# Turning input and output tiles of a one-layer decoder step with VectorE block transposes instead of TensorE transposes

## The reference

```
h  = rmsnorm(x) ; z = h @ w_in                       # 2048 x 10240, columns for r k v g u g_pool gate_a gate_b
decay = exp(-0.6065 * sigmoid(w0 + tanh(xw @ w1) @ w2))   # low rank 96, xw mixes h and the previous row
a     = sigmoid(a0 + (xa @ a1) @ a2)                      # low rank 96
S, o  = wkv7_scan(...)                               # 16 heads of 64
m  = sigmoid(gate_a) * (y_a @ w_branch[0]) + sigmoid(gate_b) * (y_b @ w_branch[1])
x  = x + rmsnorm(m @ w_out)                          # 2048 x 2048
x  = x + sigmoid(x @ w_ple_gate) * (p @ w_ple)       # 2048 x 2048 and 256 x 2048
return x (tokens as rows), states
```

## Time and profile before

| | |
|---|---|
| median of 3 runs | 1179.3 us (1177.43 to 1180.31) |
| profiled execution | 1180.21 us, span 1178.6 us |
| mean granted TensorE clock | 0.993 of full speed |
| TensorE busy | 1155.0 us (98%) |
| VectorE busy | 788.6 us (67%) |
| ScalarE busy | 531.7 us (45%) |

### The profile page before, as it was taken

One profiled execution on the slowest core, in us unless ns is written; L12 is line 12 of the kernel. 1 busy time (PEld: TensorE's weight loads), 2 busy tenths in 40 slices (PEclk: granted clock), 3 DMA queues, 4 the chain that ended last, 5 costly groups with the idle time before them and its releaser, 6 DMA issues.

```text
span 1178.6 us, 22183 instructions
## 1 busy us (share of the span) xinstructions
PE 1155.0 (98%) x7876; PEld 1122.9 (95%) x7876; DVE 788.6 (67%) x1689; ACT 531.7 (45%) x906; POOL 149.8 (13%) x251
## 2 busy tenths in 40 slices
PE   6979999999999999999999999999999999999998
PEld 6869999999999999999999999999999999989998
DVE  5977898989888888888679644444444444475442
ACT  5434564646463646455363333333333433354332
POOL 2322130303012121311050000000000400000000
PEclk9989999999999999999999999999999999999999
DMA  9713343434334344333364555545555954425551
GB/s 240 186 36 102 109 110 107 111 107 111 107 99 120 98 119 117 101 108 99 113 184 124 161 144 157 145 143 158 144 151 151 280 161 139 133 69 142 165 164 47
DMA packets 279707, 155.08 MB, mean 132 GB/s; under 512 B 7717, under 2 KB 275661, under 8 KB 279012
## 3 DMA queue, kind: packets, MB, share of 16 engines
q1 hardware_dynamic: 272528, 139.65, 42.2%
q0 software_dynamic: 6992, 14.87, 4.9%
q10 hardware_dynamic: 148, 0.04, 0.0%
HBM read 149.15 MB, written 5.61 MB: 131 GB/s over the span
## 4 chain that ended last, share of the span: by engine, by line
PE 94%; DVE 3%; DMA 1%; issue 1%; POOL 0%; ACT 0%; SPq 0%; DVEq 0%; ACTq 0%; POOLq 0%
PE acc L1722 20%; PE acc L1723 19%; PE acc L1724 19%; PE wide L1724 5%; PE wide L1723 5%; PE wide L1722 5%; PE wide L1741 2%; PE wide L1823 1%; PE wide L2113 1%; PE wide L1877 1%; PE wide L1858 1%; DVE wl L1089 1%; PE wide L1864 1%; DMA xt<-in_x_prompt 1%; PE wide L1945 1%; PE wide L1869 1%
## 5 line engine op out<-in xcount | busy, mean ns | idle before, releaser
L1089 DVE TENSOR_TENSOR wl<-wraw,wh 128x1024 fp32r<-128x1024 f32 x256 | 316.9, 1244 | 196.2 <-ACT wh L708 194.2
L708 ACT CAST wh<-wraw 128x1024 fp32r<-128x1024 f32 x256 | 267.0, 1049 | 214.2 <-PE acc L1724 128.5
L1722 PE MATMUL acc<-hh,wh 128*128 128x320 f32 (+1 forms) x1084 | 349.5, 322 | 1.9 <-DVE hl L1175 1.9
L1723 PE MATMUL acc<-hl,wh 128*128 128x320 f32 (+1 forms) x1084 | 337.5, 311 | 0.0
L1724 PE MATMUL acc<-hh,wl 128*128 128x320 f32 (+1 forms) x1084 | 336.9, 311 | 0.0
L1722 PEld LDWEIGHTS acc<-hh,wh 128*128 128x128 f32 x1084 | 205.3, 189 | 2.7 <-DVE hl L1175 2.4
L1723 PEld LDWEIGHTS acc<-hl,wh 128*128 128x128 f32 x1084 | 205.0, 189 | 0.2
L1724 PEld LDWEIGHTS acc<-hh,wl 128*128 128x128 f32 x1084 | 204.9, 189 | 0.0
L1722 PE MATMUL acc<-x1h,wh 128*128 128x320 f32 x256 | 81.0, 316 | 0.0
L1722 PE MATMUL acc<-mh,wh 128*128 128x320 f32 x256 | 80.5, 315 | 0.0
L1724 PE MATMUL acc<-x1h,wl 128*128 128x320 f32 x256 | 79.1, 309 | 0.0
(11 more groups left out here) (422 smaller groups left out, 2100.6 us busy)
## 6 DMA issues: line engine op xcount, KB each, us to landing
wraw<-in_w_in SPq DMA_DIRECT2D x160, 512.0 KB, 3.8
wraw<-in_w_branch SPq DMA_DIRECT2D x32, 512.0 KB, 3.9
wraw<-in_w_out SPq DMA_DIRECT2D x32, 512.0 KB, 4.0
wraw<-in_w_ple_gate SPq DMA_DIRECT2D x32, 512.0 KB, 4.1
xt<-in_x_prompt SPq DMA_DIRECT2D x2, 1024.0 KB, 7.4
S0n<-in_state_wkv POOLq DMA_DIRECT2D x64, 32.0 KB, 4.5
out<-so POOLq DMA_DIRECT2D x16, 128.0 KB, 3.6
xt<-in_x_prompt POOLq DMA_DIRECT2D x2, 1024.0 KB, 6.9
```

Source lines behind the costliest of these rows:

```text
L708: A.copy(wh[:, slot, :], wraw[:, slot, :]).then_inc(s["hi_ready"], 1)
L1089: V.tensor_tensor(wl[:, slot, :], wraw[:, slot, :], wh[:, slot, :].bitcast(F32), ALU.subtract).then_inc(s["lo_ready"], 1)
L1722: M.matmul(out[:, 0:width], wh[:, slot, wcol], hi, start=first, stop=False)
L1723: M.matmul(out[:, 0:width], wh[:, slot, wcol], lo, start=False, stop=False)
```

## The change

It has three parts. In the start stage the first head pair's decay maps become two plain fp32 matmuls, `lora_high(0)` and `lora_low(0)` go, and VectorE's order changes. In the out stage x is turned by 40 VectorE block transposes (a 32-row quadrant by 16 k tiles by 32 columns each), three ahead of each out tile i = 2..14 and one ahead of the last, and neither TensorE nor ScalarE takes part any more (the embedding's two tiles stay with them, ahead of the last two out tiles). In the gate stage each `yo` is turned into `ytk` by sixteen VectorE block transposes right behind it; `tokens` and `token_tile` go. The stores stay where they are on SyncE and wait for sixteen block transposes. Before it writes `ytk[:, m]`, VectorE waits that all earlier stores out of it have landed.

```diff
+BLOCK_MOVES = [(a, q, r) for a in range(3) for q in range(4 if a < 2 else 2) for r in range(4)]
+TURNED = {i: BLOCK_MOVES[3 * (i - 2):3 * (i - 1)] for i in range(2, KT)}
...
             def store(i, m):
-                sp.wait_ge(s["ytk_ready"], i * 2 + 2)
+                sp.wait_ge(s["ytk_ready"], i * 16 + 16)
...
         @block.scalar
-            lora_high(0)
...
             decays(0)
             gates(4)
+            act.wait_ge(s["filled"], 2 + 10)
...
                 act.wait_ge(s["chunk_used"], i * 2 + (BASE_GATE + 2))
+                act.wait_ge(s["yo_ready"], i - 1)
                 A.activation(g3[:, m, :], acc[m][:, 0:T], ACT.Sigmoid).then_inc(s["g3_ready"], 1)
...
         @block.vector
+            values_turned(0, 3)
+            decays(0)
             dve.wait_ge(s["filled"], 2 + 10)
             states_turned(0)
             dve.wait_ge(s["lora_tok"], 4)
+            dve.wait_ge(s["lora2_ps"], 1)
             V.tensor_tensor(t1_l[:, :], t1[:, :], t1_h[:, :].bitcast(F32), ALU.subtract).then_inc(s["lora_lo"], 1)
             V.tensor_tensor(la_l[:, :], la[:, :], la_h[:, :].bitcast(F32), ALU.subtract).then_inc(s["lora_lo"], 1)
-            lora_low(0)
-            values_turned(0, 3)
-            decays(0)
...
+            def turned_blocks(a, q, r):
+                rows_q, rows_r = slice(BLK * q, BLK * (q + 1)), slice(BLK * r, BLK * (r + 1))
+                V.transpose(xTv[rows_r, :, P * a + BLK * q:P * a + BLK * (q + 1)],
+                            xt2[rows_q, a, :].rearrange("p (k d) -> p k d", d=P)[:, :, rows_r]).then_inc(s["x_turned"], 1)
+            dve.wait_ge(s["x2_in"], 48)
+            for i in range(2, KT):
+                for move in TURNED[i]:
+                    turned_blocks(*move)
+                out_tile(i // 2, i % 2)
...
                 V.tensor_tensor(yo[:, m, :], g3[:, m, :], xT[:, ds(n * (2 * T) + m * T, T)], ALU.add).then_inc(s["yo_ready"], 1)
+                if not first:
+                    dve.wait_ge(s[f"y_out{m}"], n * 32)
+                dve.wait_ge(s["yo_ready"], i + 1)
+                for q in range(4):
+                    n_tiles = 3 if q < 2 else 2
+                    for r in range(4):
+                        V.transpose(ytk[BLK * q:BLK * (q + 1), m, 0:P * n_tiles].rearrange("p (a d) -> p a d", d=P)[:, :, BLK * r:BLK * (r + 1)],
+                                    token_blocks(m, q, n_tiles)[BLK * r:BLK * (r + 1)]).then_inc(s["ytk_ready"], 1)
...
         @block.tensor
-            decay_maps(0)
+            pe.wait_ge(s["lw2_in"], 32)
+            pe.wait_ge(s["lora_tok"], 2)
+            M.matmul(B[0][:, 0:T], lw2[:, :], t1[:, :], start=True, stop=True)
+            M.matmul(B[1][:, 0:T], la2[:, :], la[:, :], start=True, stop=True).then_inc(s["lora2_ps"], 1)
...
             with pe.Fori(2, KT // 2) as n:
-                gate_tile(n, 0)
-                tokens(n * 2 - 1, 1, n * 4 - 4)
-                gate_tile(n, 1)
-                tokens(n * 2, 0, n * 4 - 2)
-            tokens(KT - 1, 1, 2 * KT - 4)
+                for m in range(2):
+                    pe.wait_ge(s["g3_ready"], n * 2 + m - 1)
+                    gate_tile(n, m)
```

More of the change, by code:

```diff
@@ L370, in build @@
         wple = r5.take("wple", [P, 2, 2 * P])
-        yo = r5.take("yo", [P, 2, T])
+        yo_wide = r5.take("yo_wide", [P, 2, 3 * P])
+        yo = yo_wide[:, :, 0:T]
         emb = at(used["ml"][0], "emb", [P, EMB, T])
@@ L1010, in _ @@
                 act.wait_ge(s["sacc_ready"], i - 1)
-                for u in TURNED[i]:
-                    turned_tile(u)
+                if i >= KT - 2:
+                    turned_embedding(i - (KT - 2))
                 square_tile(i // 2, i % 2)
@@ L1050, in gate_tile @@
                 act.wait_ge(s["chunk_used"], i * 2 + (BASE_GATE + 2))
+                act.wait_ge(s["yo_ready"], i - 1)
                 A.activation(g3[:, m, :], acc[m][:, 0:T], ACT.Sigmoid).then_inc(s["g3_ready"], 1)
[L1053 to L1059, removed]
             first_gate(0)
             first_gate(1)
-            token_tile(0, 0)
             gate_tile(1, 0)
-            token_tile(1, 1)
             gate_tile(1, 1)
-            token_tile(2, 0, 32)
             with act.Fori(2, KT // 2 - 1) as n:
-                gate_tile(n, 0)
-                token_tile(n * 2 - 1, 1, n * 32 - 32)
-                gate_tile(n, 1)
[L1072 to L1078, removed]
+                for m in range(2):
+                    gate_tile(n, m)
+            for m in range(2):
+                gate_tile(KT // 2 - 1, m, last=True)
         @block.vector
@@ L1651, in _ @@
             out_tile(0, 1)
-            with dve.Fori(1, KT // 2) as n:
-                for m in range(2):
-                    out_tile(n, m)
+            xTv = xT[:, :].rearrange("p (k t) -> p k t", t=T)
+            def turned_blocks(a, q, r):
[7 more added lines that the diff above has]
+                out_tile(i // 2, i % 2)
+            dve.wait_ge(s["x_turned"], len(BLOCK_MOVES))
             def gate_ahead(j):
@@ L2073, in _, with turned_embedding @@
             sizes = (P, P, NB * TB)
[L2075 to L2089, removed]
+            def turned_embedding(k):
+                pe.wait_ge(s["pool_in"], 64)
+                for t in range(3):
+                    last = transpose(B[4 + k][:, P * t:P * t + sizes[t]], pt[0:sizes[t], t, P * k:P * (k + 1)])
+                last.then_inc(s["pT_ps"], 1)
             for i in range(2, KT):
-                for u in TURNED[i]:
-                    turned_tile(u)
+                if i >= KT - 2:
+                    turned_embedding(i - (KT - 2))
                 out_tile(i // 2, i % 2, True)
@@ L2098, in gate_tile @@
                     chunk(n * 4 + BASE_GATE, 2 * m + h, acc[m], x1h, x1l, T, T, KC * h, h == 0, h == 1)
-            def tokens(i, m, free):
-                pe.wait_ge(s["yo_ready"], i + 1)
-                if free is not None:
-                    pe.wait_ge(s["ytk_ready"], free)
-                for t in range(3):
-                    last = transpose(B[2 + m][0:sizes[t], P * t:P * (t + 1)], yo[:, m, P * t:P * t + sizes[t]])
-                last.then_inc(s["yt_ps"], 1)
             def embedding(i):
@@ L2141, in _ @@
                 chunk(BASE_GATE, 4 + h, acc[0], x1h, x1l, T, T, KC * h, h == 0, h == 1)
[L2142 to L2144 removed]
+            pe.wait_ge(s["g3_ready"], 2)
             gate_tile(1, 1)
[L2146 removed]
             with pe.Fori(2, KT // 2) as n:
[L2148 to L2152 removed]
+                for m in range(2):
+                    pe.wait_ge(s["g3_ready"], n * 2 + m - 1)
+                    gate_tile(n, m)
 OUTS = [((1, TP, D), "float32"), ((NB, TB, D), "float32"), ((1, 1, 16, HD, HD), "float32"), ((1, 1, D), "float32"),
```

34 lines of the change are left out of this document (13 added, 21 removed).

## The result

The changed kernel takes **1211.05 us** (median of 4 runs, 1207.65 to 1212.08) against 1179.22 for the kernel before on the same chip: a ratio of 1.0266, interval 1.0243 to 1.0290. It is slower by about 32 us; 1207.5 was forecast. The profiled execution took 1211.03 us, span 1209.4, with a mean granted clock of 0.982.

The account below looks back on a forecast made before the run. TensorE, busy 98% of the span, was taken as the bound. Span 1178.6 - 8.2 (start) - 9.7 (out) + 45.7 (gate) = 1206.4; with 1.6 around it 1208, stated as 1207.5 us, range 1188 to 1224.

Parts of the forecast that it names:

- Start, forecast -8.2: Start stage: sum matmul 9.3 us earlier without TensorE's idle gap, 1.15 us given back later; net -8.2 us.
- the first L1877: Start stage: this instruction, waiting for work behind the scores, was taken to have no slack, giving back 1.15 us.
- both are just in time: Start stage: split of chunk 11 ends at 86.1, needed at 86.4; low part follows at 86.6; gain priced in full.
- Out, forecast -9.7: Out stage: sixteen turned tiles leave TensorE, 9.7 us saved; VectorE's added 2.2 us per tile stays hidden, tiles 7.04 us.
- Gate, forecast +45.7: Gate stage: sixteen VectorE transposes per tile and a wait for stores make tiles 10.9 us apart, +45.7 us.
- the ring: Gate stage: transposes 4.5, split 1.25, store 5.05 from split to landing, wake-up 0.1; 10.9 us per tile.
- the sign: Gate stage, profile after: VectorE idle 2.5 us before each group of sixteen transposes from tile 2 on.
- Clock: Gate stage: some 6.5 us at half speed takes 3.3 us of TensorE's idle gap; hidden but for 0 to 2 us.
- overlap of transposes: Gate stage rival: transposes overlap, 3.2 us per tile, short wait, TensorE is the bound; about 1160 us; 6%.
- the wait bound: Gate stage: VectorE's transposes wait for the store to land, for tiles 2 to 12.
- neither a quicker nor a slower ring: Gate stage rivals: quicker, 9.3 us a tile, 1190 us, 17%; slower, 12.6 us a tile, 1227 us, 12%.
- the first rival: Gate stage: the store wait does not bind, round 8.3 us, 1179.5 us in all, no change; 5%.

Follow-up runs that it names:

- e5: Changed kernel with each pair of stores issued one `load_gate` call (two chunk loads) earlier on SyncE: 1176.55 us.
- e6: Changed kernel with three `ytk` buffers in place of two, SyncE's order kept: 1176.89 us.
- e3: Kernel before with the start stage's part of the change alone: 1171.86 us, ratio 0.9938 to the kernel before.
- e4: Kernel before with the start and out parts of the change, gate stage as before: 1162.87 us, ratio 0.9858 to the kernel before.
- e7: Changed kernel with eight of the sixteen transposes per gate tile left out from tile 2 on: 1182.48 us.
- e9: Kernel before with the start and out parts, plus even gate tiles turned by VectorE and odd ones by TensorE: 1167.56 us.
- e11: e9 with the stores issued one `load_gate` call (two chunk loads) earlier on SyncE: 1160.03 us.

## Why the prediction was right

**Direction and mechanism.** What it named is there: the store behind the load behind the split, the wait from tile 2 to tile 12, TensorE idle and waiting for `wl`. The removal of either link (e5, e6) returned 34 us.

**Start, forecast -8.2.** The last stream matmul to the sum matmul took 22.09 us (74.04 to 96.13) and takes 13.30 (75.10 to 88.40): -8.8. At out tile 1 the kernel is 6.97 us earlier than before (929.05 then, 922.08 now), although this execution reached the end of the first stream 1.06 us later; so -8.0. About 0.8 us was given back on the way, 1.15 was priced; that it happens at the first L1877, as the step says, was not tested. By whole runs the part is worth 5 to 9 us (e3). The step "both are just in time" was wrong: `kf` was lengthened by GpSimd, the split came late, and TensorE waited 0.55 us for it (9.3 forecast, 8.8 measured). That the term as a whole still fits is luck, since about as much less was given back behind it.

**Out, forecast -9.7.** The stage from tile 1 to tile 15 went from 109.65 us (929.05 to 1038.70) to 99.81 (922.08 to 1021.89): -9.84. Transposes of 702 ns and 2.17 us for three are as priced, and the tile is 7.04.

**Gate, forecast +45.7.** From `yo` of tile 0 to the end of the span it was 109.37 us (from 1069.23) and is 156.83 (from 1052.57): +47.5. Of the 1.8 us that were missing, 0.35 lie ahead of tile 2's transposes, and 1.4 in ten rounds of 11.04 on average instead of 10.9: the transposes were right (4.51 us from 268 and 238 ns; 269 and 236 forecast), the landing in the ring took 3.84 and not 3.6 + 0.1. VectorE idled 2.9 to 3.3 us before each group, 2.5 was named as the sign. The end, from tile 12's transposes to the span's end, was forecast as 28.0 us and took 28.0.

**Clock.** The window of two rounds in the changed kernel, and one of the same stage in e5 (columns as in the earlier trace rows):

```profile
1110.00:1132.00 22.00, 17.75 (x97) 17.22 (x98) 14.68 (x41) 4.93 (x6) 0.00 (x0) 0.84 0.40 110
```

```profile
1110.00:1134.00 24.00, 21.82 (x146) 21.04 (x145) 21.86 (x60) 7.61 (x9) 0.00 (x0) 1.00 0.53 150
```

With TensorE's gaps the granted clock is 0.84 in the mean: full level in part of a round, and 0.50 for some 3 us behind each gap (1111 to 1114 here). Where TensorE waits for under 1 us a tile, it stays at 1.00. As forecast it cost nothing that can be seen, since TensorE was not the one waited for: the ring's five terms, none of them TensorE's, give the whole round. What it took out of the gap was mis-sized, without effect on the time: TensorE was idle for 4.25 of these 22 us, 2.1 a tile and not 3.8; at full clock it would have been 4.0 (11.07 - 7.04), so half clock took some 1.9 us of it and not 3.3.

**The rivals.** No overlap of transposes (x16 in 4.51); the wait bound; neither a quicker nor a slower ring. The kernel of the first rival, a round without the store's wait, is e5: 8.02 us a tile and 1176.6 us in all, where the prediction had 8.3 and 1179.5 (two splits in a row take 2.36 us and not 2.5). The sum of the three stages' measured changes, 47.5 - 9.84 - 6.97 = 30.7, is the growth of the span, 30.8. The measured span is 3.0 us over the forecast one of 1206.4: 1.8 in the gate stage, 1.06 by the later start of this execution, the rest in the two small terms.

## What to carry to other kernels

When work moves to another engine, look for what that engine's progress releases, not only for its load: here a store stood in a queue behind a load that waited for the very engine that then waited for the store, and that ring cost 34 us (e5), against some 14 for VectorE's longer work (e5 against e4). Its mark is an engine's idle time that stays the same when its work is cut (e7), and it is opened by the order in the queue (e5) or one more buffer (e6). A slow path that does not fit into every tile may fit into every second one, once the queue behind it is in order (e9 against e11).

## What the hardware showed that I had not expected

A VectorE and a GpSimd instruction on on-chip memory held each other up: in the five pairs shown, whichever began second ended late. GpSimd's 128x512 multiplication `zr`, 1.21 to 1.28 us when it began first, made a 0.44 us VectorE instruction take 1.18, a 1.22 us split 2.08 and a 0.49 us one 1.35; begun after a split, it took 1.79 or 1.96 itself. The held instruction ended 0.2 to 1.1 us after the holder, never before. The Trainium skill, SBUF — State Buffer, "SBUF: two separate sides", calls this an exclusive lock on a port pair shared by the two engines, in which the loser fully blocks. The rows agree with that in all five cases; which of the page's conditions `kf`, a tensor with per-partition scalars, fulfils, no row shows. Not every pair did so: beside GpSimd's last memset in the changed kernel (78.14 to 79.09) VectorE's transposes of 32x160 kept their 0.33 us.
